# First attention of a three-layer transformer kernel: bias rows requested earlier, two modulation quarters in front of the heads, row sums in the odd filler steps

## What is computed

```python
c_act = silu(c)
mod = c_act @ w_ada + b_ada                     # (1024) x (1024 x 6144): 12 column blocks of 512
sh_m, sc_m, gt_m, sh_f, sc_f, gt_f = split(mod, 6)
h = rms_norm(x, g_mix) * (1 + sc_m) + sh_m
qa, ka, va, qb, kb, vb, gate_logits = split(h @ w_in, ...)   # blocks of 512 columns
oa = moba_attention(qa, ka, va, rel_bias)       # 8 heads of 64; softmax of q k / 8 + bias by distance
ob = stick_breaking_attention(qb, kb, vb)       # 8 heads of 64
mixed = (sigmoid(g_a) * (oa @ w_br_moba) + sigmoid(g_b) * (ob @ w_br_sb)) @ w_out
x = x + gt_m * mixed                            # then h2 from sc_f, sh_f, and the feed-forward part with gt_f
```

## Time and profile before

| | |
|---|---|
| Median of 3 runs | 1410.62 us (1409.11 to 1411.71) |
| The profiled execution's own time | 1411.21 us |
| Its span in the trace | 1409.5 us |
| PE busy | 1375.7 us, 98% of the span |
| DVE busy | 1096.6 us, 78% |
| ACT busy | 817.3 us, 58% |
| POOL busy | 80.7 us, 6% |
| Mean granted PE clock | 0.992 |

### The profile page before, as it was taken

How to read it: one execution, slowest core, us unless ns; L and a number is a source line. 1 busy time by engine, 2 the same in 40 slices (tenths; PEclk the granted TensorE clock), 3 DMA queues, 4 the chain that set the end, 5 groups by cost and what they waited for, 6 DMA issues and landing times.

```text
span 1409.5 us, 19422 instructions
## 1 busy us (share of the span) xinstructions
PE 1375.7 (98%) x6957; PEld 1143.3 (81%) x6957; DVE 1096.6 (78%) x1563; ACT 817.3 (58%) x1305; POOL 80.7 (6%) x133
## 2 busy tenths in 40 slices
PE   6999999999999999999899999999999999999998
PEld 5878877999987888887678888888888877788886
DVE  6577787799767999669986999569996556779893
ACT  4556755755446466466576566465655566566562
POOL 3011100000000000012300000000000100000000
PEclk8999999999999999999999999999999999999999
DMA  9887555487553574635255566735747373564560
GB/s 352 300 292 252 194 178 182 146 282 258 189 194 127 193 239 162 236 131 171 98 169 170 174 220 208 239 106 197 249 152 263 118 222 120 178 221 131 203 239 30
DMA packets 160702, 274.37 MB, mean 195 GB/s; under 512 B 5953, under 2 KB 87617, under 8 KB 160609
## 3 DMA queue, kind: packets, MB, share of 16 engines
q1 hardware_dynamic: 153904, 250.86, 52.2%
q0 software_dynamic: 5552, 20.20, 4.6%
q10 hardware_dynamic: 1153, 2.07, 0.4%
HBM read 272.05 MB, written 1.06 MB: 194 GB/s over the span
## 4 chain that ended last, share of the span: by engine, by line
PE 73%; DVE 7%; issue 2%; ACT 1%; DMA 1%; POOL 0%; DVEq 0%; POOLq 0%; ACTq 0%; SPq 0%
PE psum L2825 18%; PE psum L2827 17%; PE psum L2826 17%; PE psum L3080 3%; PE psum L3081 3%; PE psum L3082 3%; PE psum L2868 2%; PE psum L2867 2%; PE psum L2865 2%; DVE w_lo L2360 2%; PE psum L3106 1%; PE psum L2930 1%; DVE lo_at L2360 1%; PE psum L3002 1%; DVE lo_qk L2360 1%
## 5 line engine op out<-in xcount | busy, mean ns | idle before, releaser
L2360 DVE TENSOR_TENSOR w_lo<-raw,w_hi 128x1024 fp32r<-128x1024 f32 (+2 forms) x310 | 368.0, 1231 | 70.6 <-ACT w_hi L2091 69.5
L2091 ACT ACTIVATE w_hi<-raw 128x1024 fp32r<-128x1024 f32 (+2 forms) x310 | 307.9, 1047 | 94.0 <-DMA raw<-in_ffn_wu_dram 25.3
L2825 PE MATMUL psum<-w_hi,hT_hi 128*128 128x512 f32 x712 | 287.4, 404 | 3.2 <-DVE hT_lo L2522 1.2
L2826 PE MATMUL psum<-w_lo,hT_hi 128*128 128x512 f32 x712 | 278.9, 392 | 0.0
L2827 PE MATMUL psum<-w_hi,hT_lo 128*128 128x512 f32 x712 | 278.9, 392 | 0.0
L2825 PEld LDWEIGHTS psum<-w_hi,hT_hi 128*128 128x128 f32 x712 | 135.0, 190 | 35.8 <-issue 7.1
L2827 PEld LDWEIGHTS psum<-w_hi,hT_lo 128*128 128x128 f32 x712 | 134.9, 190 | 29.1
L2826 PEld LDWEIGHTS psum<-w_lo,hT_hi 128*128 128x128 f32 x712 | 135.1, 190 | 25.8 <-issue 0.5
L2825 PE MATMUL psum<-w_hi,hc_hi 128*128 128x512 f32 x272 | 106.7, 392 | 0.9 <-DVE hc_lo L2744 0.6
L2827 PE MATMUL psum<-w_hi,hc_lo 128*128 128x512 f32 x272 | 106.0, 390 | 0.0
L2826 PE MATMUL psum<-w_lo,hc_hi 128*128 128x512 f32 x272 | 106.0, 390 | 0.0
(11 more groups left out here) (301 smaller groups left out, 2871.6 us busy)
## 6 DMA issues: line engine op xcount, KB each, us to landing
raw<-in_ffn_wd_dram SPq DMA_DIRECT2D x44, 1024.0 KB, 4.8
raw<-in_ffn_wg_dram SPq DMA_DIRECT2D x56, 512.0 KB, 3.9
raw<-in_ffn_wu_dram SPq DMA_DIRECT2D x56, 512.0 KB, 5.4
raw<-in_w_up_dram SPq DMA_DIRECT2D x44, 512.0 KB, 4.8
raw<-in_w_in_dram SPq DMA_DIRECT2D x19, 1024.0 KB, 7.6
raw<-in_ffn_wg_dram SPq DMA_DIRECT2D x16, 1024.0 KB, 5.1
raw<-in_ffn_wu_dram SPq DMA_DIRECT2D x16, 1024.0 KB, 5.2
ada_raw<-in_w_ada_dram POOLq DMA_DIRECT2D x24, 512.0 KB, 5.3
```

The lines of the kernel that those rows point to most:

```text
L2091: nc.scalar.activation(hi_of(s)[:, cs], source_of(s)[:, cs], ACT.Copy).then_inc(ready, 1)
L2360: nc.vector.tensor_tensor(lo_of(u)[:, cs], source_of(u)[:, cs], hi_of(u)[:, cs].bitcast(F32), ALU.subtract)\
L2825: nc.tensor.matmul(o, a_hi, b_hi, start=start, stop=False)
L2826: nc.tensor.matmul(o, a_hi, b_lo, start=False, stop=False)
```

## The change

The request for the bias rows waits for an earlier unit (3, the first unit of va, in place of 5, the second of ka). q0 and q1 stand in front of the heads: q0 behind the bias request, q1 in front of the first filler. In a filler, the projection's step, with its splits, now stands in front of the quarter. The sums stand in the odd fillers. With two quarters in front, the heads hold seven more, and the stick-breaking heads three in place of five.

```diff
     pl.add("late_loads")
-    pl.add("load_bias", which=0, after=("unit_used", ka[1][-1]["unit"] + 1))
+    pl.add("load_bias", which=0, after=("unit_used", va[1][0]["unit"] + 1))
+    quarter()
     r["va"], last = va[0], va[1][-1]
     pl.split_ahead(last["unit"])
...
-    fa = [[sum_next, quarter, f] for name in ("qb", "kb", "vb") for f in heads_of[name]]
-    fa += [[sum_next, turn_second], [quarter], [sum_next]]
+    quarter()
+    fa = []
+    for name in ("qb", "kb", "vb"):
+        first, second = heads_of[name]
+        fa += [[first, quarter], [sum_next, second, quarter]]
+    fa += [[turn_second], [sum_next, quarter], []]
...
-    fb = [[quarter, gates[0][0]], [sum_low, gates[0][1]], [], [quarter, gates[1][0]], [sum_low, gates[1][1]], [],
-          [quarter, gates[2][0]], [sum_low, gates[2][1]], [], [quarter, gates[3][0]], [sum_low, gates[3][1], turn_moba], [],
-          [quarter, second_branch], [first_branch]]
+    fb = [[quarter, gates[0][0]], [sum_low, gates[0][1]], [], [quarter, gates[1][0]], [sum_low, gates[1][1]], [],
+          [quarter, gates[2][0]], [sum_low, gates[2][1]], [], [gates[3][0]], [sum_low, gates[3][1], turn_moba], [],
+          [second_branch], [first_branch]]
```

## The result

| | before | after |
|---|---|---|
| Median | 1410.82 us (1409.11 to 1411.71, 4 runs) | 1419.29 us (1416.90 to 1419.77, 4 runs) |
| Ratio after / before | | 1.0055, 95% interval 1.0042 to 1.0068 |
| The profiled execution | 1411.21 us, span 1409.5 us | 1419.00 us, span 1417.3 us |

The changed kernel is slower by about 8 us. The forecast was 1410.2 us with a range up to 1412.9; it was wrong, and none of its rivals reached this far.

The account below looks back on a forecast made before the run. PE, busy 98% of the span, was taken as the bound. A wait for q9 (+0.45) and -0.81 at `w_out` made -0.36 us; the profiled 1410.85, less 0.6 for the median, gave 1410.2 us, range 1407.4 to 1412.9.

Parts of the forecast that it names:

- it comes after both copies and the sum ... +0.75: Last heads: with sum 7 there, the product with v starts later and takes in a wait of 0.32; +0.75 us (0.5 to 1.2).
- the row at 2.66 us: Earlier trace, wait ending at 695.80: the clock stayed at 1.00, so no fall was assumed in a 2.7 us wait.
- The other sums are in time: q3 (88.4): Sums 5, 6, 7: q3, q5, q7 end at 88.4, 103.1, 117.9, ahead of PE at 90.7, 106.4, 119.0; no wait.
- my upper bound: Landing of q1's load: 11.2 us as for the bias rows, so q1 ends at 76.0 in place of 73.7.
- Only the end of q9 counts: First gate's sum 8: PE waits 2.7 us for q9 (132.6), so earlier gains and losses on PE drop out; +0.45 us.
- the rival of a late q1: q1 ends at 76.0, PE waits 5.0 us for q9 and the clock falls: +3.5, 1414.1 us; chance 0.12.
- Splits in front of quarters ... nothing is gained: DVE order in a filler: same splits, each ready earlier against PE's need, nothing waited on them; no gain.
- the order inside a round does not change this: Chain of quarters: request, landing and reading in one buffer are in series, so the pace stays 7.36 us per quarter.
- the 4.74 us at sum 4: Before sum 4, a 3.18 us gap of PE and 1.56 us of low clock behind it go: 4.74 us gained.
- the stalls behind transposes in the rounds: Sums 5 and 6 directly behind a pair's transposes wait for ACT's copy: 0.88 us each, +1.76 us.
- forecast -0.81: Product with `w_out`: the sum that stood there is gone, saving 0.81 us.
- nothing gained from the logits' wait for bias rows: First logits: the 4.81 us DVE wait for bias rows goes, but was no gap of PE; worth nothing by itself.

Follow-up runs that it names:

- e11: e1 with the sums in the odd fillers, quarters and splits as before: 1413.07 us, ratio 1.0013 to the kernel before.
- e9: The changed kernel with the quarter in front of the splits again: 1416.92 us, ratio 1.0041 to the kernel before.
- e14: The changed kernel with seven eighths of each quarter's weights behind q0 left out of the loads: 1415.04 us, ratio 1.0025 to the kernel before.
- e2: The changed kernel with the sums of the moba heads one filler sooner, in the even fillers: 1422.74 us, ratio 1.0076 to the kernel before.
- e3: The changed kernel with ScalarE's late loads issued some 18 us sooner: 1419.44 us, ratio 1.0047 to the kernel before.
- e5: e1 with the splits in front of the quarter in each filler, quarters and sums unmoved: 1417.04 us, ratio 1.0032 to the kernel before.
- e13: The changed kernel with sum 7 out of the last full pair, q7 left ahead of its logits: 1416.66 us, ratio 1.0046 to the kernel before.
- e6: The changed kernel with q7 behind the last full pair's logits, sums 7 and 8 one place later: 1412.92 us, ratio 1.0008 to the kernel before.
- e1: The kernel before with only the early request for the bias rows: 1407.76 us, ratio 0.9963 to the kernel before.
- e8: e1 with sum 7 three fillers later in the stick-breaking heads: 1408.24 us, ratio 0.9974 to the kernel before.
- e7: The changed kernel with sums 4 to 7 one filler later, quarters unmoved: 1418.93 us, ratio 1.0053 to the kernel before.
- e10: The changed kernel with the quarter in front of the splits again and with e6's move of q7: 1414.07 us, ratio 1.0019 to the kernel before.

## Why the prediction was wrong, step by step

**The step that failed most is the tail: "it comes after both copies and the sum ... +0.75".** I took sum 7's place behind the last full pair's transposes as its own 0.81 us and a shift of short waits. It measured +5.83 in the changed kernel and +4.0 in e11, where the edit stands without early quarters (there it is sum 6). What I left out is the clock. In the kernel before, the last pair's short waits (0.25, 0.41, 0.32) leave it at 1.00. With 0.25 and 0.80 (e9, e11, e14) or 0.25 and 1.13 (after) it goes to 0.50 for 8 to 10 us. I looked for a fall only behind a wait near 3 us. Nor was the row at 2.66 us a safe ground for that: the same wait stands in all 16 profiles at 2.63 to 2.68 us, and in the 6 us behind it the granted clock fell in ten of them and stayed at 1.00 in six (before, after, e2, e3, e5, e13). From e6, where the three transposes take 0.88 us in place of the 0.52 of the earlier trace rows:

```profile
696.44 0.88 PE L3008 MATMUL psum<-cst,attn 128*128 128x128 f32 x3 [2.65 <-DVE attn L2619]
```

**The second is "The other sums are in time: q3 (88.4)".** q3 ended at 94.08 and sum 5 waited 2.31 us, with a low clock behind it (94.18 to the product with v at 102.20 is 8.02 us; the same steps took 6.45 in the earlier trace rows). Two sizes were off. The second half of q1 took about 9.5 us in place of 6.9, inside my bounds, and q1 ended at 77.36, which less the start's 1.44 is 75.9, my upper bound. And the next two quarters took 16.7 us in place of 14.7. I applied a pace read from a kernel in which the quarters begin later, when ScalarE's late loads are through; e14 gives 0.9 to 3.2 us to the landings. In e6 and e13 the same sum waits 1.48 and 1.47 us and the clock holds, so this step is a wait of 1.5 us in those profiles, and one of 2.3 with a fall of 1.6 behind it in this one.

**"Only the end of q9 counts" was wrong in kind.** PE never waited at sum 8: at 140.17 it has no bracket, since q9 was done at 138.52. The losses lay ahead of it, and they did not drop out. So the rival of a late q1 had q1's end right (76.0) and its path wrong: its wait of 5.0 us at this sum never came. (Its limit of 75.3 for q1 doesn't follow from the forecast's own sums either: a wait of 3.18 us there needs q1 at about 74.3.)

**"Splits in front of quarters ... nothing is gained" and "the order inside a round does not change this"** treated DVE's order as free. e5 puts its price at 0.7% in the kernel with the early bias request. The quarter had been done in the time in which DVE waited for ScalarE's part of the split. In the changed kernel, with two quarters in front, undoing it brings nothing that can be measured (e9): a split then waits behind q2, whose load is late.

**Not weighed at all:** that q7 now stands ahead of the last full pair's logits. The order of DVE shows it. I had used it for round 0 and not looked at the end. Without the sum behind the transposes it is 3.60 us of PE waiting (e13); with the sum there it adds 0.3 us to a wait, and the tail is as slow without it (e14).

**Right:** the 4.74 us at sum 4 (4.8 in e1's rounds, 3.9 in e8's); the stalls behind transposes in the rounds, where a sum that needn't wait for its quarter starts 1.45 us after them (e9, e11, e14), as forecast; -0.80 at `w_out`, forecast -0.81 (from the first matmul behind `hT_lo` to the transposes 6.37 us before, 5.57 after); nothing gained from the logits' wait for bias rows.

Put together from the kernels: early bias request -0.37%, sums in odd fillers +0.50% (e11 over e1), q0 and q1 in front with the splits ahead of quarters, and no sum behind the last pair's transposes, about -0.05% (e6 over e11), q7 ahead of the last pair's logits with sum 7 behind them +0.47% (after over e6). That makes 0.55%. The first two and the last are beyond the intervals; the third is not, and as it takes a cost out and puts others in, it doesn't show that the two quarters in front are free.

## What to carry to other kernels

When an edit moves work between engines' queues, look at every place where the moved piece now stands, at the end of the loop as well as at its head, and ask what is queued behind it: here a quarter in front of the last logits (e13 against e6, 0.38%, 5.4 us) cost more than the stall that the change removed. An engine's wait in the middle of its queue is a place to put work in, and whoever moves the waiting instruction ahead of that work loses it. Waits of about a microsecond on TensorE were followed by up to ten microseconds of half clock here, so a sum of stalls should carry the clock as a case of its own even where no single wait is long, and the parts of a change should be tried singly: one line of four held all the gain.

## What the hardware showed beyond that

**The clock falls without a long wait.** In the tail no single bracket was above 1.13 us and the granted clock still went to 0.50. In the kernel before, a wait of 2.66 us left it at 1.00. The length of a wait doesn't settle it, since behind that same wait it fell in ten of the 16 profiles, nor does a second wait close by: in e1 it fell behind a single wait of 1.01 us, with none in the nine microseconds before; in the rounds of e6 waits of 1.48 and 1.17 left it at 1.00, and of e5's waits of 1.28 and 1.27 us the second brought it down and the first did not. What decides stays open. The Trainium skill (TensorE: Matmul & The Clock Gate, section A second HAM failure mode: psum-queue depth-cycling) tells of a kernel whose short idle times between groups of matmuls, and not one long one, swing the clock. These runs agree in so far as the clock fell behind waits of 1.13 us and less; that the cause is the same they don't show.

**The start differs at the same instructions.** Up to the first turns of ka all kernels give PE the same matmuls, and those turns came between 60.8 and 64.7 us in 16 profiles (60.94 in e7 and 64.73 in e11, so not by whether quarters stand in front). It is the clock: the same three groups in the timeline of PE take 0.99 to 1.07 us before and 1.71 to 1.95 after. In the seven profiles that have the long ones (after, e2, e3, e6, e10, e11, e14) the turns come at 62.8 to 64.7, in the nine others at 60.8 to 62.6.

```profile
15.27 0.99 PE L2878 MATMUL psum<-c_act,QK 128*128 128x1 f32 x8
16.13 1.03 PE L2916 MATMUL psum<-ones,ada_acc 128*128 128x1 f32 x8
17.02 1.07 PE L2930 MATMUL psum<-cst,scr 128*128 128x128 f32 x8
```

```profile
15.54 1.71 PE L2883 MATMUL psum<-c_act,QK 128*128 128x1 f32 x8
17.11 1.84 PE L2921 MATMUL psum<-ones,ada_acc 128*128 128x1 f32 x8
18.82 1.95 PE L2935 MATMUL psum<-cst,scr 128*128 128x128 f32 x8
```

The record of the granted clock says 1.00 there in the changed kernel, though the matmuls take what they take at 0.50 (1.95 for the same group in the kernel before at 44.18, where the record says 0.50), and each group starts that much later. Where a row's duration and that record differ, the duration is to be believed. The Trainium skill (TensorE: Matmul & The Clock Gate, section Seeing it yourself) warns that such records are not always reliable; this case agrees, with 1.95 us under a record of 1.00. For the reader it means that two spans with a difference of 2 us, one profile each, are not a comparison: cut the trace at common instructions, or take medians.
